# The last token tile of the two fullest experts held as high and low halves side by side

## The reference, cut to what matters

```python
logits = (t @ w_router).astype(jnp.float32)
top_val, top_idx = lax.top_k(logits, TOP_K)          # TOP_K = 2
top_w = jax.nn.softmax(top_val, axis=-1)
combine = jnp.sum(jax.nn.one_hot(top_idx, N_EXPERTS) * top_w[..., None], axis=1)
for e in range(N_EXPERTS):                            # 8 experts
    y_e = swiglu_ffn(t, w_gate_up[e], w_down[e])      # (silu(t@Wg) * (t@Wu)) @ Wd, inner width 1408
    out = out + combine[:, e:e + 1] * y_e
```

## Time and profile before

| what | value |
|---|---|
| median of 3 runs | 2823.86 us (2818.79 to 2825.7) |
| the profiled execution, its own time | 2822.24 us |
| span of the profiled execution, first to last instruction | 2820.9 us |
| mean granted TensorE clock | 0.986 of full speed |
| TensorE busy | 2680.6 us, 95% of the span |
| VectorE, ScalarE busy | 58%, 43% of the span |

### The profile page before, as it was taken

One profiled execution on the slowest core, in us unless ns is written; L12 is line 12 of the kernel. 1 busy time (PEld: TensorE's weight loads), 2 busy tenths in 40 slices (PEclk: granted clock), 3 DMA queues, 4 the chain that ended last, 5 costly groups with the idle time before them and its releaser, 6 DMA issues. The chain is left out here.

```text
span 2820.9 us, 34134 instructions
## 1 busy us (share of the span) xinstructions
PE 2680.6 (95%) x13693; PEld 2192.7 (78%) x13693; DVE 1636.2 (58%) x2675; ACT 1210.9 (43%) x1969; POOL 185.7 (7%) x252
## 2 busy tenths in 40 slices
PE   6999999999999898899999998999999999999998
PEld 5777788887887787688877776787788767788887
DVE  6786564555773674544488887433325487553444
ACT  3666322223435343333477775422324356332222
POOL 0000000000002630200000010121100001000001
PEclk8999999999999999899999999999999999999999
DMA  6233264433232220535599994221321115222222
GB/s 241 87 126 124 90 225 150 155 142 105 90 127 77 61 72 29 210 114 185 195 351 349 363 365 157 90 92 68 127 90 53 60 57 201 75 101 86 105 86 71
DMA packets 87253, 391.65 MB, mean 139 GB/s; under 512 B 21482, under 2 KB 25614, under 8 KB 51342
## 3 DMA queue, kind: packets, MB, share of 16 engines
q1 hardware_dynamic: 73680, 353.53, 34.7%
q10 hardware_dynamic: 10382, 25.87, 2.6%
q0 software_dynamic: 3024, 9.98, 1.0%
HBM read 369.02 MB, written 25.57 MB: 140 GB/s over the span
## 5 line engine op out<-in xcount | busy, mean ns | idle before, releaser
L343 DVE TENSOR_TENSOR wlo<-stage,whi 128x1024 fp32r<-128x1024 f32 (+3 forms) x481 | 513.0, 1105 | 324.9 <-ACT whi L355 322.8
L355 ACT ACTIVATE whi<-stage 128x1024 fp32r<-128x1024 f32 (+3 forms) x481 | 437.3, 956 | 214.0 <-PE ps L695 189.7
L695 PE MATMUL ps<-whi,mxhi 128*128 128x512 f32 (+1 forms) x528 | 204.3, 387 | 9.9 <-DVE wlo L343 7.8
L695 PE MATMUL ps<-bxhi,whi 128*128 128x512 f32 x480 | 198.9, 414 | 8.7 <-DVE y0lo L343 4.0
L695 PE MATMUL ps<-whi,mxlo 128*128 128x512 f32 (+1 forms) x528 | 197.6, 374 | 0.0
L695 PE MATMUL ps<-wlo,mxhi 128*128 128x512 f32 (+1 forms) x528 | 197.6, 374 | 0.0
L695 PE MATMUL ps<-bxhi,wlo 128*128 128x512 f32 x480 | 189.0, 394 | 0.0
L695 PE MATMUL ps<-bxlo,whi 128*128 128x512 f32 x480 | 188.5, 393 | 0.0
L343 DVE TENSOR_TENSOR wlo<-more,whi 128x1024 fp32r<-128x1024 f32 (+1 forms) x126 | 142.8, 1175 | 58.7 <-ACT whi L355 58.2
L355 ACT ACTIVATE whi<-more 128x1024 fp32r<-128x1024 f32 (+1 forms) x126 | 121.6, 1014 | 49.7 <-PE ps L695 44.8
L695 PE MATMUL ps<-lxhi,whi 128*128 128x512 f32 x352 | 140.4, 399 | 1.6 <-DVE lxlo L351 1.6
(11 more groups left out here) (633 smaller groups left out, 5977.6 us busy)
## 6 DMA issues: line engine op xcount, KB each, us to landing
stage<-in_gu SPq DMA_DIRECT2D x92, 1024.0 KB, 6.2
more<-in_gu SPq DMA_DIRECT2D x40, 1024.0 KB, 6.9
stage<-in_ada SPq DMA_DIRECT2D x39, 1024.0 KB, 4.8
stage<-in_dn SPq DMA_DIRECT2D x19, 1024.0 KB, 6.0
stage<-in_dn SPq DMA_DIRECT2D x24, 768.0 KB, 4.2
stage<-in_gin SPq DMA_DIRECT2D x16, 1024.0 KB, 4.8
stage<-in_gt SPq DMA_DIRECT2D x16, 1024.0 KB, 4.9
more<-in_dn SPq DMA_DIRECT2D x13, 1024.0 KB, 5.4
```

The source lines that it names most:

```text
L343: return e.do.tensor_tensor(out, x, y, op)
L355: return e.do.activation(out, x, f, **kw)
L695: return self.p.do.matmul(out, lhsT, rhs, start=start, stop=stop, skip_group_check=True)
```

## The change

In `FEW`, the last tile of expert 0 and of expert 1 may hold at most 64 tokens; the limits become 320 and 192 tokens. Such a tile (`small`) keeps the high parts of its 64 tokens in columns 0 to 63 of its place in `L.X[0]` and `L.H[0]`, and the low parts in columns 64 to 127. One matmul with all 128 columns against the high weights gives high by high in PSUM rows 0 to 63 and low by high in rows 64 to 127; a second with the first 64 columns against the low weights adds high by low to rows 0 to 63. Rows 64 to 127 are then added to rows 0 to 63: ScalarE copies the upper rows to SBUF (`L.sums`, an unused part of `L.X`), VectorE adds the lower ones, and only then comes silu, or the output. Transposes of a small tile take 64 rows. The zero filling gets two DMAs more, of 64 rows each.

```diff
+HALVED = [1, 1, 0, 0, 0, 0, 0, 0]
...
-    c["lim"] = np.broadcast_to(128 * np.array(FEW) + 0.5, (P, 8))
+    c["lim"] = np.broadcast_to(128 * np.array(FEW) - 64.0 * np.array(HALVED) + 0.5, (P, 8))
...
+        blank += [(BASE[r] + FEW[r] * P - 64, 64) for r in range(8) if HALVED[r]]
...
+        L.sums = [pair[0:64, n // 2, 4 * (n % 2):4 * (n % 2) + 4, 3 * P:4 * P] for n in range(4)]
... (experts_pe, gather)
-                        k = self.tr(ps[:, (m - q) * P:(m - q + 1) * P], L.rows[i % 3][:, m * P:(m + 1) * P])
+                        k = self.tr(ps[:, (m - q) * P:(m - q) * P + w], L.rows[i % 3][0:w, m * P:(m + 1) * P], self.c("ident")[0:w, 0:w])
... (experts_pe, turn)
-                        k = self.tr(ps[:, o:o + P], L.gate[L.z[r, j, t] % 4][:, i * P:(i + 1) * P])
+                        k = self.tr(ps[:, o:o + wide], L.gate[L.z[r, j, t] % 4][0:wide, i * P:(i + 1) * P], self.c("ident")[0:wide, 0:wide])
... (gate and up pieces)
+                        if self.small(r, t, tiles):
+                            z = self.pe_small(ps, hi[:, q, :], lo[:, q, :], L.X[0][:, k0 + q, :], t * P, k0 + q == 0, k0 + q == 7)
+                            continue
                         self.mm(ps, L.X[0][:, k0 + q, s], hi[:, q, :], k0 + q == 0, False)
                         self.mm(ps, L.X[0][:, k0 + q, s], lo[:, q, :], False, False)
                         z = self.mm(ps, L.X[1][:, k0 + q, s], hi[:, q, :], False, k0 + q == 7)
... (down pieces: the same with L.H and k0 + q == 10)
+    def small(self, r, t, tiles):
+        return tiles is FEW and HALVED[r] == 1 and t == tiles[r] - 1
+
+    def pe_small(self, ps, hi, lo, X, at, first, last):
+        both, high = X[:, at:at + P], X[:, at:at + 64]
+        if not last:
+            self.mm(ps, both, hi, first, False)
+        z = self.mm(ps[0:64], high, lo, False, False)
+        return self.mm(ps, both, hi, False, True) if last else z
... (experts_act, after a gate and up group)
+                        if self.small(r, t, tiles):
+                            sums = L.sums[j % 2][:, 0:2 * w, :]
+                            act(a, sums, self.bank(use)[64:128, 0:256 * w].rearrange("p (b f) -> p b f", f=P), ACT.Copy).then_inc(*A.up(("c", r, j, t)))
+                            a.wait_ge(V(("c", r, j, t)))
+                            act(a, L.gate[k % 4][0:64, 0:w * P].rearrange("p (b f) -> p b f", b=w), sums[:, 0:2 * w:2, :], ACT.Silu).then_inc(*A.up(("s", r, j, t)))
+                            continue
... (experts_act, after a down half)
+                    if self.small(r, t, tiles):
+                        act(a, L.sums[2 + m], self.bank(use)[64:128, :].rearrange("p (b f) -> p b f", f=P), ACT.Copy).then_inc(*A.up(("dc", r, m)))
+                        a.wait_ge(V(("dc", r, m)))
+                        a.do.dma_start(self.d["yrows"][a0:a0 + 64, 512 * m:512 * m + 512], dst[0:64, :]).then_inc(*y.up(("y", r, m, t), by=16))
+                        continue
... (experts_dve, after a gate and up group)
+                        if self.small(r, t, tiles):
+                            sums = L.sums[j % 2][:, 0:2 * w, :]
+                            v.wait_ge(A(("c", r, j, t)))
+                            tt(v, sums, self.bank(use)[0:64, 0:256 * w].rearrange("p (b f) -> p b f", f=P), sums, ADD).then_inc(*V.up(("c", r, j, t), free(use)))
+                            up = sums[:, 1:2 * w:2, :]
+                            v.wait_ge(A(("s", r, j, t)), V.now())
+                            tt(v, s[0:64], s[0:64], up, MUL).then_inc(*V.up(("z", r, j, t)))
+                            continue
... (experts_dve, in the down pieces)
+                if i % 3 == 2 and self.small(r, n - 1, tiles):
+                    m, use = i // 3, ("dn", r, i // 3, n - 1)
+                    k = L.y[r, m, n - 1]
+                    v.wait_ge(A(("dc", r, m)), *([self.Dy[k % 4](("y", *L.ykeys[k - 4]))] if k >= 4 else []))
+                    blocks = lambda ap: ap.rearrange("p (b f) -> p b f", f=P)
+                    tt(v, blocks(L.out[k % 4][0:64, :]), blocks(self.bank(use)[0:64, :]), L.sums[2 + m], ADD).then_inc(*V.up(("dc", r, m), free(use)))
```

More of the change, by code:

```diff
@@ L1476, in ffn0_act @@
         self.pin("silu_and_others")
-        blank = [BASE[r] + n * P for r in range(8) for n in range(FEW[r], TILES[r])] + [BASE[7]]
+        blank = [(BASE[r] + n * P, P) for r in range(8) for n in range(FEW[r], TILES[r])] + [(BASE[7], P)]
+        blank += [(BASE[r] + FEW[r] * P - 64, 64) for r in range(8) if HALVED[r]]
         def between(e, j):
@@ L1483, in between @@
             elif 0 < n <= len(blank):
-                a0 = blank[n - 1]
-                a.do.dma_start(self.d["yrows"][a0:a0 + P, :], self.d["zero"]).then_inc(*self.Dz[n].up("blank", by=16))
+                a0, w = blank[n - 1]
+                a.do.dma_start(self.d["yrows"][a0:a0 + w, :], self.d["zero"][0:w]).then_inc(*self.Dz[n].up("blank", by=16))
         self.ffn_act(L, 0, lambda m: self.act_square("f0", m, L.tmp[0:2], 1.0, *([self.P("xs2")] if m == 0 else [self.V(((0, 1), "l", 10))])), between)
@@ L2659, in gather @@
                     p.wait_ge(*vacant)
+                    w = 64 if self.small(r, t, tiles) else P
                     for m in range(q, q + 4):
-                        k = self.tr(ps[:, (m - q) * P:(m - q + 1) * P], L.rows[i % 3][:, m * P:(m + 1) * P])
+                        k = self.tr(ps[:, (m - q) * P:(m - q) * P + w], L.rows[i % 3][0:w, m * P:(m + 1) * P], self.c("ident")[0:w, 0:w])
                     k.then_inc(*P_.up(("x", r, t, q)))
@@ L2672, in turn @@
                         o = ((i - half) * n + t) * P
-                        k = self.tr(ps[:, o:o + P], L.gate[L.z[r, j, t] % 4][:, i * P:(i + 1) * P])
+                        wide = 64 if self.small(r, t, tiles) else P
+                        k = self.tr(ps[:, o:o + wide], L.gate[L.z[r, j, t] % 4][0:wide, i * P:(i + 1) * P], self.c("ident")[0:wide, 0:wide])
                 k.then_inc(*P_.up(use))
@@ L2721, in experts_pe @@
                             p.wait_ge(wt(q), V(("hl", r, k0 + q)))
+                            if self.small(r, t, tiles):
+                                z = self.pe_small(ps[:, :], hi[:, q, :], lo[:, q, :], L.H[0][:, k0 + q, :], t * P, k0 + q == 0, k0 + q == 10)
+                                continue
                             self.mm(ps[:, :], L.H[0][:, k0 + q, s], hi[:, q, :], k0 + q == 0, False)
@@ L2744, in gather @@
                         a.wait_ge(P_(("w", self.place[f"gu1_{r - 1}", 10])))
-                    act(a, L.X[0][:, q:q + 4, t * P:(t + 1) * P], self.bank(use)[:, :].rearrange("p (m n) -> p m n", m=4), ACT.Copy).then_inc(*A.up(("xh", r, t, q)))
+                    w = 64 if self.small(r, t, tiles) else P
+                    act(a, L.X[0][:, q:q + 4, t * P:t * P + w], self.bank(use)[:, :].rearrange("p (m n) -> p m n", m=4)[:, :, 0:w], ACT.Copy).then_inc(*A.up(("xh", r, t, q)))
         def turn(r, j):
@@ L2752, in turn @@
                     a.wait_ge(P_(("w", self.place[f"dn1_{r - 1}", 5])))
-                src = self.bank(use)[:, 0:w * n * P].rearrange("p (i f) -> p i f", i=w)
-                act(a, L.H[0][:, 2 * j + half:2 * j + half + w, 0:n * P], src, ACT.Copy).then_inc(*A.up(("hh", *use[1:])))
+                cols = n * P - (64 if self.small(r, n - 1, tiles) else 0)
+                src = self.bank(use)[:, 0:w * n * P].rearrange("p (i f) -> p i f", i=w)[:, :, 0:cols]
+                act(a, L.H[0][:, 2 * j + half:2 * j + half + w, 0:cols], src, ACT.Copy).then_inc(*A.up(("hh", *use[1:])))
         def pair(c):
@@ L2798, in experts_act @@
                     a.wait_ge(P_(use))
+                    a0 = BASE[r] + t * P
+                    if self.small(r, t, tiles):
[3 more added lines that the diff above has]
+                        continue
                     if k >= 4:
@@ L2801, in experts_act @@
                     act(a, dst, self.bank(use)[:, :], ACT.Copy).then_inc(*A.up(free(use)))
-                    a0 = BASE[r] + t * P
                     a.wait_ge(A.now())
@@ L2812, in gather @@
                     use = ("x", r, t, q)
-                    h, l = (x[:, q:q + 4, t * P:(t + 1) * P] for x in L.X)
+                    w = 64 if self.small(r, t, tiles) else P
+                    h = L.X[0][:, q:q + 4, t * P:t * P + w]
+                    l = L.X[0][:, q:q + 4, t * P + w:t * P + P] if w < P else L.X[1][:, q:q + 4, t * P:(t + 1) * P]
                     v.wait_ge(A(("xh", r, t, q)))
-                    tt(v, l, self.bank(use)[:, :].rearrange("p (m n) -> p m n", m=4), h.bitcast(F32), SUB).then_inc(*V.up(("xl", r, t, q), free(use)))
+                    tt(v, l, self.bank(use)[:, :].rearrange("p (m n) -> p m n", m=4)[:, :, 0:w], h.bitcast(F32), SUB).then_inc(*V.up(("xl", r, t, q), free(use)))
         def turn(r, j):
@@ L2822, in turn @@
                 src = self.bank(use)[:, 0:w * n * P].rearrange("p (i f) -> p i f", i=w)
+                if self.small(r, n - 1, tiles):
```

(7 more changed lines are left out.)

## The result

The change made the kernel faster: 2799.39 us median (2798.43 to 2801.29, 4 runs) against 2821.32 us (2814.75 to 2825.7, 4 runs: the three of the table ahead and one more), ratio 0.9929 with a 95% interval of 0.9914 to 0.9944. In a second measurement, with six more runs, it was 0.9924 (0.9912 to 0.9937). The forecast was 2845 us with a range of 2833 to 2858 and a chance of 0.07 for faster: wrong in sign.

The account below looks back on a forecast made before the run. TensorE was taken to set the pace alone in experts 0 and 1. 49.8 us added against 30.1 saved (+19.7), plus 1.9 on other engines, gave +21.6 on the 2823.86 median: 2845 us, range 2833 to 2858.

Parts of the forecast that it names:

- What bounds the kernel: In experts 0 and 1 TensorE alone sets the pace; their gain or loss moves everything behind them by as much.
- The side that runs, and the 30.1 us removed: The `FEW` side stays, with 11 tiles; two small tiles lose one of three matmuls per step, saving 30.1 us.
- What it adds on TensorE: In small tiles, changes between 64- and 128-wide matmuls and transposes cost 49.8 us against 30.1 saved: +19.7 us.
- 248 changes between S and its neighbours: Switches into and out of the small tile's 64-column second matmul (high by low): 18.2, 23.3 and 1.2 us.
- Rival 1: The forms cost nothing: a 64-column matmul runs as a full one with idle columns; 2796 us, chance 0.06.
- The transposes, 48 x 0.147 = 7.1: At turns and gathers of experts 0 and 1, 48 changes between small and full transposes cost 7.1 us.
- The other engines, +1.9: Around small tiles, ScalarE and VectorE work adds waits and a shorter gather saves some: +1.9 us in sum.
- The wait at expert 2's second piece: At expert 1's end ScalarE first waits for VectorE's sum before splitting weights that TensorE awaits: +0.8 us.
- The waits before the last turns: At the last group the extra copy and add are exposed: some 0.6 us in expert 0, 1.0 in expert 1.
- The wait behind expert 0's small gather: At expert 0's start the small tile's gather is split at half width: -0.5 us.
- Groups 0 to 4: Their turn comes one piece later, 4.5 us or more of matmuls, which hides the longer chain of sums.
- rival 3: In small tiles the clock falls to 1.2 GHz and streaming time doubles: about 2900 us, chance 0.04.

Follow-up runs that it names:

- experiment 2: Changed kernel with the small tile's second matmul in plain float32: 2882.76 us with 128 stationary columns (wide), 2924.13 us with 64 (narrow).
- experiment 3: Changed kernel with 64-column float32 second matmuls, these grouped together within each piece of a small tile instead of in turns: 2893.04 us, ratio 1.026.
- experiment 1: Changed kernel with the small tile's second matmul taking all 128 stationary columns, still in the rounded type: 2794.5 us, ratio 0.9913.
- experiment 5: Changed kernel with a small tile's transposes taking all 128 rows in place of 64: 2794.62 us, ratio 0.991.
- experiment 6: Changed kernel with ScalarE's wait for VectorE's sum and the send of a small tile's result moved behind the next piece's splits: 2798.32 us, one run.

## Why the prediction was wrong, step by step

- **What bounds the kernel: right.** TensorE alone sets experts 0 and 1, and what they gained moved everything behind them: the 22.9 us arrived at the end but for 0.9.
- **The side that runs, and the 30.1 us removed: right.** The count fell by 140 matmuls.
- **The failed step: "What it adds on TensorE", the 42.7 us for 248 changes between S and its neighbours.** The price was read from plain float32 matmuls and put on matmuls of the rounded type. For float32 it was right to 5% (40.8 us in experiment 2, and 31 forecast against 29.7 in experiment 3); for the rounded type it is nothing (experiment 1 against the result), but for some 0.009 us a step. The form column shows rows and columns in use, and the type isn't in it: both kinds are written `f32`. What could be seen before was that the rows carry "x2", two passes, and the expert's matmuls one. The prediction said "eight groups of two float32 passes" and didn't ask whether that mattered. The trace before couldn't have settled it: all 32 of its matmuls of form 128*64 are of that two-pass kind. Rival 1 named the right outcome, 2796 us, but the prediction argued against it from PSUM rows, which were not the difference, and gave it 0.06. Why the rounded type is exempt stays open: the runs show that it is, not what in the array makes it so.
- **The transposes, 48 x 0.147 = 7.1: right in kind, 5.1 in size.** The trace after has starts 0.20 apart at the changes in place of 0.11, and experiment 5 takes them away. In the eight full turns a change costs 0.13, near the 0.147 that was taken. Over all 48 it is 5.1 / 48 = 0.106, for two reasons: the 64-row transposes of the gathers are faster among themselves, which the prediction left out, and the waits before the last turns are shorter where the transposes ahead of them are slower.
- **The other engines, +1.9: half of it.** The wait at expert 2's second piece grew by 0.82 (0.8 forecast), and experiment 6 shows the queue behind it. The waits before the last turns grew by some 0.2 in expert 0 and 0.3 in expert 1 (0.6 and 1.0 forecast); with the faster transposes of experiment 5 they are some 0.1 us longer again in each, so the slower transposes cover a part of them; what covers the rest isn't shown. The wait behind expert 0's small gather was shorter by 0.3 (0.5 forecast). Groups 0 to 4 show no wait, as said.
- **The clock** stayed at 1.00 from 1175 to 1430 us; rival 3 had no part in it.

The wait before expert 1's last turn is in two pieces after the change, 1.07 us together in place of 0.73:

```profile
1356.56 0.33 PE L699 MATMUL ps<-small,mtmp 128*128 128x128 f32 x1 [0.41 <-DVE mtmp L344]
1357.54 0.27 PE L699 MATMUL ps<-small,mtmp 64*128 64x64 f32 x1 [0.66 <-DVE mtmp L344]
```

With the sizes as measured the sum closes: -30.1 + 5.1 + 1.3 + 1.0 = -22.7, against -22.9. The 5.1 of experiment 5 already has some 0.2 us of waits in it, so the terms are known to a few tenths and the close fit is in part luck.

The Trainium skill, "TensorEngine Tiling (Array Packing)", Key Properties, was cited for changes of tiling mode draining TensorE. Two kinds of change here have such a cost: 0.165 us each for float32 with 64 columns, and 0.13 for 64-row transposes. A rounded matmul with 64 columns has none of that size, 0.228 and 0.235 between starts, and which instructions change the mode no trace here shows.

## What to carry to other kernels

Before a price is moved from one stage to another, compare everything that the instruction has, the type of its operands and its passes too, and not only the shape that the trace prints; where they differ, give the transfer itself a chance, larger than 0.06. A half-empty tile with high and low parts side by side saves a third of its matmuls; its matmuls, and its transposes where they stand by turns with full ones, are best left at the full 128 columns and rows, since narrowing saved nothing there. Narrow transposes that stand together, as in a gather, did no harm here. An engine's wait for another's result belongs behind the work that others wait for.

## What the runs showed of the hardware

- A float32 matmul with 64 stationary columns between others of 128 costs 0.165 us per change of width (40.8 us for 248); one of the rounded type costs no more than 1.3 us for the same 248.
- The price is on the change: 34 in place of 124 per tile gave back 29.7 us, and six fewer per head in the second block 0.85 us of 2.81.
- Transposes of 64 rows by turns with those of 128 cost 0.13 us per change (0.53 for the four of a turn). Eight of them in a row start 0.063 us apart, where eight of 128 rows start 0.109 apart.
- With the rounded type and 512 columns moving, a step took 0.461 us with a 64-column matmul in it and 0.453 with 128 columns throughout (medians of 88). The cause of these 8 ns stays open.
